# One product per unit of the narrow feed-forward parts issued in two column pieces

## The chip, the cores and the metric

The kernel runs on one core of one Trainium2 chip. The metric is the device time of one execution in microseconds (us).

## What is computed

Two transformer-like blocks run one after the other on one sequence of 256 tokens with 1024 channels. The first has four layers, each with a mixer (retention, convolution, dilated attention, retention) and a gated feed-forward part; the second has two layers over 272 tokens (16 tokens are put ahead), each with a mixer and a wider feed-forward part. The change is in the feed-forward parts of the first block, four times this:

```python
DEPTH = 4
FFN_HIDDEN = -(-8 * D_MODEL // (3 * 256)) * 256          # 2816

def _swiglu(h, w_in, w_out):
    a = h @ w_in
    return (jax.nn.silu(a[..., :FFN_HIDDEN]) * a[..., FFN_HIDDEN:]) @ w_out

def first_block(x, ...):
    for i in range(DEPTH):
        hn = _rmsnorm(x, norm_w[i, 0])
        ...
        x = x + _rmsnorm(m, norm_w[i, 1])
        f = _swiglu(_rmsnorm(x, norm_w[i, 2]), ffn_w_in[i], ffn_w_out[i])
        x = x + _rmsnorm(f, norm_w[i, 3])
    return x
```

## The kernel before, in words

Activations lie with channels on the 128 partitions and tokens (256, or 272 in the second block) along the columns. Every dense matrix is a `Phase`: it is cut into units, and a unit is `tiles` weight tiles of 128x128 that are multiplied into one output of 128 channels. For each layer of the first block there are two feed-forward phases, whose names begin with `ffn`: `ffn_in` with 44 units of 8 tiles (gate and value rows in pairs), and `ffn_out` with 16 units of 11 tiles, two units per output. The second block's feed-forward phases are called `mlp_in` and `mlp_out`; they stream 272 columns and are not touched.

SyncE (SP) loads one unit's weights at a time into a ring of raw slots. ScalarE (line 1313) rounds four tiles at a time to `weights_hi` (type fp32r), VectorE (line 2155) puts the remainder into `weights_lo`, and adds to the semaphore `split_ready`. The activations are split likewise into a high and a low part. TensorE then makes each dense product out of three fp32r products, in `product`: hi by hi (line 526), weight hi by activation lo (line 527), and weight lo by activation hi (line 528), all accumulated in the same PSUM bank. The stationary operand is the 128x128 weight tile, the moving one the activations of all 256 tokens.

`multiply` runs one unit: for each tile k it calls `product`, waits on `split_ready` at every fourth tile, and tells the splitting engines through `sub_multiplied` when four tiles are done. In `ffn_in` the first four units go through `first_units`, tile by tile as the normalised activations arrive, which calls `product` by itself; the other 40 units go through `multiply`, four of them in `turn(1, False)` and 36 in a hardware loop of nine rounds with four units each. `ffn_out` goes through `dense` in four rounds of four units. The order on each engine is that of the code; semaphores alone tie the engines together.

Other products in the kernel (attention scores, norm sums, transposes) have F32 operands, not fp32r. The filler `keep_busy` (line 520) and line 578 are such.

Of the kernel before, what the change touches and what calls it, by code (L numbers as in the profile page):

```python
# [44 lines left out]
SLOTS = 4  # L45
SUB = 4
SUBS = 4
SLOT_TILES = 11


# [151 lines left out]
def build(nc, dram, out, const_at):  # L202
# [3 lines left out]
    with ExitStack() as ctx:  # L206
        def sb(name, shape):
            return ctx.enter_context(nc.sbuf_tensor(name, shape, F32))

        def sbr(name, shape):  # L210
            return ctx.enter_context(nc.sbuf_tensor(name, shape, F32R))
# [4 lines left out]

        raw = [sb(f"weights{s}", [P, SLOT_TILES, P]) for s in range(SLOTS)]
        w_hi = [sbr(f"weights_hi{s}", [P, SUB, P]) for s in range(SUBS)]
        w_lo = [sbr(f"weights_lo{s}", [P, SUB, P]) for s in range(SUBS)]
        h = sb("h", [P, DC, S2])  # L220
# [293 lines left out]
        def _(pe):  # L514
# [4 lines left out]
                for _ in range(n):  # L519
                    nc.tensor.matmul(PS[:, bank, 0:S1], mean, rope_cos[:, 0:S1], start=True, stop=True)  # L520

            def product(acc, hi, lo, src, first, last):


                src_hi, src_lo = src
                nc.tensor.matmul(acc, hi, src_hi, start=first, stop=False)  # L526
                nc.tensor.matmul(acc, hi, src_lo, start=False, stop=False)  # L527
                return nc.tensor.matmul(acc, lo, src_hi, start=False, stop=last)  # L528

            def multiply(phase, i, u, acc, src, ready=None):  # L530


                for k in range(phase.tiles):
                    kk = (u % phase.upo) * phase.tiles + k
                    sub = u * phase.sps + k // SUB
                    if k % SUB == 0:
                        pe.wait_ge(split_ready, i * (phase.body * phase.sps) + (phase.sub0 + sub + 1))
                    if ready:
                        pe.wait_ge(*ready(kk))
                    last = product(acc, w_hi[sub % phase.subs][:, k % SUB, :], w_lo[sub % phase.subs][:, k % SUB, :], src(kk),  # L540
                                   kk == 0, kk == phase.upo * phase.tiles - 1)
                    if k % SUB == SUB - 1 or k == phase.tiles - 1:
                        last.then_inc(sub_multiplied, 1)

            def dense(phase, src, n, free, first_free, ready, begin=0):


                body = phase.body
                banks = SLOTS if phase.upo == 1 else 2
                with pe.Fori(begin, phase.units // body) as i:  # L550
                    for u in range(body):
                        o = u // phase.upo
                        if phase.pairs:
                            if u % 2 == 0:
                                pe.wait_ge(free, i * (body // 2) + (first_free + u // 2))
                        elif u % phase.upo == 0:
                            pe.wait_ge(free, i * (body // phase.upo) + (first_free + o))
                        multiply(phase, i, u, PS[:, o % banks, 0:n], src, ready if u < phase.upo else None)

            def last_outputs(phase, src, n):  # L560

                for u in range(phase.body):
                    multiply(phase, 1, u, PS[:, 4 + u, 0:n], src)
# [27 lines left out]
            def first_units(phase, src, ready, acc=lambda u: PS[:, 4 + u, 0:S1]):  # L591

                for c in range(DC):
                    pe.wait_ge(split_ready, phase.sub0 + c + 1)
                    pe.wait_ge(*ready(c))
                    for u in range(4):
                        last = product(acc(u), w_hi[c % phase.subs][:, u, :], w_lo[c % phase.subs][:, u, :], src(c),
                                       c == 0, c == DC - 1)
                    last.then_inc(sub_multiplied, 1)
# [12 lines left out]
            def ret_queries(phase, layer, src, ready):  # L612
                first_units(phase, src, ready)
                pe.wait_ge(out_evacuated, FREE_BANKS + phase.out0)
                multiply(phase, 1, 0, PS[:, 0, 0:S1], src)
                if layer == 0:
                    pe.wait_ge(consts_loaded, 16)
                input_mean(2 * layer)
                multiply(phase, 1, 1, PS[:, 1, 0:S1], src)
                multiply(phase, 1, 2, PS[:, 2, 0:S1], src)  # L620
                pe.wait_ge(rstd_ready, 4 * layer + 1)
                multiply(phase, 1, 3, PS[:, 3, 0:S1], src)
                pe.wait_ge(out_evacuated, evacuated(phase, 4))
                turn_row(2 * layer, 4)
                dense_outputs(phase, src, S1, None, 2)
# [29 lines left out]
            def retention(j, layer):  # L655
# [27 lines left out]
                def part_output(sub, o, quarter):  # L683

                    pe.wait_ge(split_ready, phase.sub0 + sub + 1)
                    for k in range(SUB):
                        pe.wait_ge(R["split"], ret_split(j, SUB * quarter + k))
                        last = product(PS[:, 4 + o, 0:S1], w_hi[sub % phase.subs][:, k, :], w_lo[sub % phase.subs][:, k, :],
                                       (ret_hi[SUB * quarter + k], ret_lo[SUB * quarter + k]),
                                       quarter == k == 0, quarter == SUB - 1 and k == SUB - 1)  # L690
                    last.then_inc(sub_multiplied, 1)
# [541 lines left out]
            def normed(number, n):  # L1233

                return (lambda k: (xn_hi[n][:, k, :], xn_lo[n][:, k, :])), (lambda k: (x_split, DC * number + k + 1))

            def hidden(hi, lo, name):
                return (lambda k: (hi[:, k, :], lo[:, k, :])), (lambda k: (part_lo, hidden0[name] + k + 1))

            for layer in range(DEPTH):  # L1240
# [6 lines left out]
                src, ready = normed(2 * layer, S1)  # L1247
# [20 lines left out]
                src, ready = normed(2 * layer + 1, S1)  # L1268
                gated_pairs(ph[f"ffn_in{layer}"], layer, src, ready)
                src, ready = hidden(hid_hi, hid_lo, f"ffn_in{layer}")  # L1270
# [3 lines left out]
            for layer in range(2):  # L1274
                src, ready = normed(2 * DEPTH + 2 * layer, S2)
# [8 lines left out]
                src, ready = normed(2 * DEPTH + 2 * layer + 1, S2)  # L1284
                dense_outputs(ph[f"mlp_in{layer}"], src, S2, ready)
                post_sum(17 + 2 * layer, S2)
                src, ready = hidden(mlp_hi, mlp_lo, f"mlp_in{layer}")
# [2205 lines left out]
```

## Time and profile before

| | |
|---|---|
| median of 2 runs | 2409.32 us (2403.69 to 2414.94) |
| the profiled execution's own time | 2417.55 us |
| its span, first to last instruction | 2415.8 us |
| mean granted TensorE clock | 0.999 |
| TensorE matmul busy | 2375.3 us, 98% of the span |
| TensorE weight load busy | 2279.6 us, 94% |
| VectorE, ScalarE busy | 1705.2 us, 1359.8 us |

Two rows of TensorE are shown: PE is the streaming of the moving operand, PEld the load of the stationary one, which can run beside the streaming of the instruction before. The duration of one PE record reaches past the start of the next, because matmuls are pipelined; what an instruction costs in a stream is the distance between two starts (called the pitch below), not its duration.

### The profile page before, as it was taken

The numbers are of one execution on the slowest core, as the hardware profiler recorded it, in microseconds if no ns is written. First come the engines' busy times: TensorE is split into PE (matmuls) and PEld (weight loads), VectorE is DVE, ScalarE is ACT, GpSimd is POOL, SyncE is SP. The second block draws the span as 40 slices with busy tenths as digits, with TensorE's granted clock in tenths as the row PEclk, the third lists the DMA queues.
The fourth block names the chain that finished last, engine by engine and source line by source line (L and its number), as shares of the span: only waits on it lengthen the run. The fifth ranks groups of instructions, "written<-read, shape, count | busy, mean of one in ns | idle before, by whom it ended". The sixth has DMA issues, their size and how long they took to land.

```text
span 2415.8 us, 55632 instructions
## 1 busy us (share of the span) xinstructions
PE 2375.3 (98%) x20004; PEld 2279.6 (94%) x20004; DVE 1705.2 (71%) x3359; ACT 1359.8 (56%) x2806; POOL 3.4 (0%) x9
## 2 busy tenths in 40 slices
PE   8999999999999999999999999999999999999998
PEld 8899999889999999999998999999899999999998
DVE  7666767877658778776576667657576776677864
ACT  5555555465556555565555565557755444566544
POOL 0000000000000000000000000000000000000000
PEclk9999999999999999999999999999999999999999
DMA  7635664335654444455655446645444555434564
GB/s 238 175 122 163 193 201 155 107 106 178 196 166 141 132 144 138 139 160 187 203 157 174 139 148 190 204 163 160 133 139 131 171 178 180 132 111 141 175 179 134
DMA packets 103400, 385.75 MB, mean 160 GB/s; under 512 B 11344, under 2 KB 13520, under 8 KB 103024
## 3 DMA queue, kind: packets, MB, share of 16 engines
q1 hardware_dynamic: 102784, 381.78, 51.1%
q0 software_dynamic: 496, 2.38, 0.3%
q8 instruction: 73, 1.20, 0.2%
q14 instruction: 47, 0.39, 0.0%
HBM read 383.07 MB, written 1.05 MB: 159 GB/s over the span
## 4 chain that ended last, share of the span: by engine, by line
PE 90%; DVE 6%; ACT 2%; issue 1%; DMA 0%; DVEq 0%; ACTq 0%; SPq 0%
PE acc L526 26%; PE acc L527 25%; PE acc L528 25%; DVE weights_lo L2155 2%; PE acc L732 1%; PE acc L734 1%; PE acc L733 1%; ACT weights_hi L1313 1%; PE acc L754 1%; PE acc L821 1%; DVE h L2304 1%; DVE y L2293 1%; DVE xn_parts L2300 1%; PE acc L844 1%; PE acc L866 1%
## 5 line engine op out<-in xcount | busy, mean ns | idle before, releaser
L2155 DVE TENSOR_TENSOR weights_lo<-weights,weights_hi 128x512 fp32r<-128x512 f32 (+1 forms) x1392 | 907.2, 682 | 405.8 <-ACT weights_hi L1313 400.6
L526 PE MATMUL acc<-xn_parts,weights_hi 128*128 128x256 f32 (+1 forms) x3456 | 986.2, 285 | 15.1 <-DVE xn_parts L2300 6.9
L527 PE MATMUL acc<-xn_parts,weights_hi 128*128 128x256 f32 (+1 forms) x3456 | 971.8, 281 | 0.0
L528 PE MATMUL acc<-xn_parts,weights_lo 128*128 128x256 f32 (+1 forms) x3456 | 971.6, 281 | 0.0
L1313 ACT ACTIVATE weights_hi<-weights 128x512 fp32r<-128x512 f32 (+1 forms) x1392 | 815.7, 620 | 259.3 <-PE acc L528 229.7
L526 PEld LDWEIGHTS acc<-xn_parts,weights_hi 128*128 128x128 f32 x3456 | 653.2, 189 | 32.0 <-issue 22.7
L528 PEld LDWEIGHTS acc<-xn_parts,weights_lo 128*128 128x128 f32 x3456 | 651.5, 189 | 0.0
L527 PEld LDWEIGHTS acc<-xn_parts,weights_hi 128*128 128x128 f32 x3456 | 650.4, 188 | 0.9
L526 PE MATMUL acc<-arena_r,weights_hi 128*128 128x256 f32 (+1 forms) x1792 | 510.0, 285 | 3.6 <-DVE arena_r L2796 1.2
L528 PE MATMUL acc<-arena_r,weights_lo 128*128 128x256 f32 (+1 forms) x1792 | 506.3, 283 | 0.0
L527 PE MATMUL acc<-arena_r,weights_hi 128*128 128x256 f32 (+1 forms) x1792 | 506.2, 282 | 0.0
L526 PEld LDWEIGHTS acc<-arena_r,weights_hi 128*128 128x128 f32 x1792 | 338.2, 189 | 6.7 <-issue 3.3
L527 PEld LDWEIGHTS acc<-arena_r,weights_hi 128*128 128x128 f32 x1792 | 337.9, 189 | 0.3
L528 PEld LDWEIGHTS acc<-arena_r,weights_lo 128*128 128x128 f32 x1792 | 337.6, 188 | 0.0
L1574 ACT ACTIVATE y<-y 128x256 f32<-128x256 f32 x88 | 35.9, 416 | 158.6 <-DVE y L2469 158.6
L2469 DVE TENSOR_TENSOR y<-acc,rstd 128x256 f32<-128x256 f32 x88 | 36.6, 423 | 73.5 <-PE acc L528 73.5
L1952 ACT ACTIVATE silu<-acc 128x272 f32<-128x272 f32 x64 | 25.5, 398 | 96.0 <-PE acc L528 95.9
L526 PE MATMUL acc<-xn_parts,arena_r 128*128 128x256 f32 (+1 forms) x256 | 74.1, 290 | 0.5 <-DVE xn_parts L2300 0.4
L528 PE MATMUL acc<-xn_parts,arena_r 128*128 128x256 f32 (+1 forms) x256 | 71.7, 280 | 0.0
L527 PE MATMUL acc<-xn_parts,arena_r 128*128 128x256 f32 (+1 forms) x256 | 71.7, 280 | 0.0
L2271 DVE TENSOR_TENSOR sum_of_squares<-sum_of_squares,sq 128x256 f32<-128x256 f32 (+1 forms) x79 | 33.9, 429 | 49.0 <-ACT sq L1399 33.9
L1755 ACT ACTIVATE arena<-acc 128x256 f32<-128x256 f32 x63 | 23.5, 374 | 62.4 <-PE acc L528 62.4
(325 smaller groups left out, 2324.3 us busy)
## 6 DMA issues: line engine op xcount, KB each, us to landing
weights<-in_ffn_in SPq DMA_DIRECT2D x176, 512.0 KB, 3.8
weights<-in_ffn_out SPq DMA_DIRECT2D x64, 704.0 KB, 4.1
weights<-in_att_in SPq DMA_DIRECT2D x72, 512.0 KB, 3.5
weights<-in_mlp_in SPq DMA_DIRECT2D x64, 512.0 KB, 3.5
weights<-in_mlp_out SPq DMA_DIRECT2D x64, 512.0 KB, 3.5
weights<-in_ret_qk SPq DMA_DIRECT2D x32, 512.0 KB, 3.9
weights<-in_ret_v SPq DMA_DIRECT2D x32, 512.0 KB, 3.7
weights<-in_ret_g SPq DMA_DIRECT2D x32, 512.0 KB, 3.5
```

Of the source, the lines that this page charges most:

```text
L526: nc.tensor.matmul(acc, hi, src_hi, start=first, stop=False)
L527: nc.tensor.matmul(acc, hi, src_lo, start=False, stop=False)
L528: return nc.tensor.matmul(acc, lo, src_hi, start=False, stop=last)
L732: nc.tensor.matmul(acc, x_hi[:, tokens], whi, start=(k == 0), stop=False)
L733: nc.tensor.matmul(acc, x_hi[:, tokens], wlo, start=False, stop=False)
L734: last = nc.tensor.matmul(acc, x_lo[:, tokens], whi, start=False, stop=(k == DC - 1))
L1313: nc.scalar.activation(w_hi[sub % phase.subs][:, 0:n, :], raw[slot][:, j * SUB:j * SUB + n, :], ACT.Copy)\
L1574: nc.scalar.activation(ffn_gate[:, slot, :], ffn_gate[:, slot, :], ACT.Silu).then_inc(gate_ready, 1)
L1952: nc.scalar.activation(silu[:, u % 2, :], PS[:, u % SLOTS, 0:S2], ACT.Relu).then_inc(out_evacuated, 1)
L2155: nc.vector.tensor_tensor(w_lo[sub % phase.subs][:, 0:n, :], raw[slot][:, j * SUB:j * SUB + n, :], w_hi[sub % phase.subs][:, 0:n, :].bitca ...
L2271: nc.vector.tensor_tensor(ssum[:, 0:n], ssum[:, 0:n], sq[:, o, 0:n], ALU.add).then_inc(y_added, 1)
L2469: nc.vector.tensor_tensor(ffn_gate[:, slot, :], acc, rstd[:, 0:S1], ALU.mult).then_inc(gate_scaled, 1)
```

## The change

`product` gets an argument `cut`. Where it is not zero, the middle product (weight hi by activation lo) is issued as two instructions with the same weight tile: one for the columns up to `cut`, one for the rest. `multiply` passes it for tile k = 2 of each unit of a phase whose name begins with `ffn`: 240 for the first unit of a round (240+16 columns), 128 for the second (128+128), 192 for the third (192+64), 252 for the fourth (252+4). The columns that are multiplied stay the same in number and content.

```diff
+CUTS = (240, 128, 192, 252)
...
-            def product(acc, hi, lo, src, first, last):
+            def product(acc, hi, lo, src, first, last, cut=0):
 
 
                 src_hi, src_lo = src
                 nc.tensor.matmul(acc, hi, src_hi, start=first, stop=False)
-                nc.tensor.matmul(acc, hi, src_lo, start=False, stop=False)
+                if cut:
+                    nc.tensor.matmul(acc[:, 0:cut], hi, src_lo[:, 0:cut], start=False, stop=False)
+                    nc.tensor.matmul(acc[:, cut:], hi, src_lo[:, cut:], start=False, stop=False)
+                else:
+                    nc.tensor.matmul(acc, hi, src_lo, start=False, stop=False)
                 return nc.tensor.matmul(acc, lo, src_hi, start=False, stop=last)
...
                     last = product(acc, w_hi[sub % phase.subs][:, k % SUB, :], w_lo[sub % phase.subs][:, k % SUB, :], src(kk),
-                                   kk == 0, kk == phase.upo * phase.tiles - 1)
+                                   kk == 0, kk == phase.upo * phase.tiles - 1,
+                                   CUTS[u] if k == 2 and phase.name.startswith("ffn") else 0)
```

TensorE in `ffn_in0`, the first unit after the tile-by-tile start, tiles 1 to 3 of its first four tiles, before (`xn_parts` are the split activations, `weights_hi0` and `weights_lo0` the first buffer of split weights):

```order
L526 MATMUL acc<-xn_parts,weights_hi0 128x256
L527 MATMUL acc<-xn_parts,weights_hi0 128x256
L528 MATMUL acc<-xn_parts,weights_lo0 128x256
L526 MATMUL acc<-xn_parts,weights_hi0 128x256
L527 MATMUL acc<-xn_parts,weights_hi0 128x256
L528 MATMUL acc<-xn_parts,weights_lo0 128x256
L526 MATMUL acc<-xn_parts,weights_hi0 128x256
L527 MATMUL acc<-xn_parts,weights_hi0 128x256
L528 MATMUL acc<-xn_parts,weights_lo0 128x256
```

The same place after the change:

```order
L527 MATMUL acc<-xn_parts,weights_hi0 128x256
L532 MATMUL acc<-xn_parts,weights_hi0 128x256
L533 MATMUL acc<-xn_parts,weights_lo0 128x256
L527 MATMUL acc<-xn_parts,weights_hi0 128x256
L529 MATMUL acc<-xn_parts,weights_hi0 128x240
L530 MATMUL acc<-xn_parts,weights_hi0 128x16
L533 MATMUL acc<-xn_parts,weights_lo0 128x256
L527 MATMUL acc<-xn_parts,weights_hi0 128x256
L532 MATMUL acc<-xn_parts,weights_hi0 128x256
L533 MATMUL acc<-xn_parts,weights_lo0 128x256
```

The middle product of tile 2 stands there as two rows of 240 and 16 columns; its neighbours are as before (lines 526, 527 and 528 are now 527, 532 and 533).

TensorE in `ffn_out0`, the fourth unit of the round, tiles 1 to 3, before (`arena_r_50` holds the split hidden activations):

```order
L528 MATMUL acc<-arena_r_50,weights_lo1 128x256
L526 MATMUL acc<-arena_r_50,weights_hi1 128x256
L527 MATMUL acc<-arena_r_50,weights_hi1 128x256
L528 MATMUL acc<-arena_r_50,weights_lo1 128x256
L526 MATMUL acc<-arena_r_50,weights_hi1 128x256
L527 MATMUL acc<-arena_r_50,weights_hi1 128x256
L528 MATMUL acc<-arena_r_50,weights_lo1 128x256
L537 REGISTER_ALU
```

The same place after the change:

```order
L532 MATMUL acc<-arena_r_50,weights_hi1 128x256
L533 MATMUL acc<-arena_r_50,weights_lo1 128x256
L527 MATMUL acc<-arena_r_50,weights_hi1 128x256
L529 MATMUL acc<-arena_r_50,weights_hi1 128x252
L530 MATMUL acc<-arena_r_50,weights_hi1 128x4
L533 MATMUL acc<-arena_r_50,weights_lo1 128x256
L527 MATMUL acc<-arena_r_50,weights_hi1 128x256
L532 MATMUL acc<-arena_r_50,weights_hi1 128x256
L533 MATMUL acc<-arena_r_50,weights_lo1 128x256
```

Here the pieces have 252 and 4 columns. In the whole program TensorE has 7345 rows written in place of 7297, 48 more: eight places in each of four `ffn_in` phases and four in each of four `ffn_out` phases. The other engines' instructions are unchanged.

## Rows read from the trace of the kernel before

**Rows 1.** Page of the profile: span, busy time, and the chain by engine and line.

```profile
span 2415.8 us, 55632 instructions
...
PE 2375.3 (98%) x20004; PEld 2279.6 (94%) x20004; DVE 1705.2 (71%) x3359; ACT 1359.8 (56%) x2806; POOL 3.4 (0%) x9
...
PE 90%; DVE 6%; ACT 2%; issue 1%; DMA 0%; DVEq 0%; ACTq 0%; SPq 0%
PE acc L526 26%; PE acc L527 25%; PE acc L528 25%; DVE weights_lo L2155 2%; PE acc L732 1%; PE acc L734 1%; PE acc L733 1%; ACT weights_hi L1313 1%; PE acc L754 1%; PE acc L821 1%; DVE h L2304 1%; DVE y L2293 1%; DVE xn_parts L2300 1%; PE acc L844 1%; PE acc L866 1%
...
```

**Rows 2.** Page, costliest groups: the three products, loads included, and both weight splits.

```profile
...
L2155 DVE TENSOR_TENSOR weights_lo<-weights,weights_hi 128x512 fp32r<-128x512 f32 (+1 forms) x1392 | 907.2, 682 | 405.8 <-ACT weights_hi L1313 400.6
L526 PE MATMUL acc<-xn_parts,weights_hi 128*128 128x256 f32 (+1 forms) x3456 | 986.2, 285 | 15.1 <-DVE xn_parts L2300 6.9
L527 PE MATMUL acc<-xn_parts,weights_hi 128*128 128x256 f32 (+1 forms) x3456 | 971.8, 281 | 0.0
...
L1313 ACT ACTIVATE weights_hi<-weights 128x512 fp32r<-128x512 f32 (+1 forms) x1392 | 815.7, 620 | 259.3 <-PE acc L528 229.7
...
L527 PEld LDWEIGHTS acc<-xn_parts,weights_hi 128*128 128x128 f32 x3456 | 650.4, 188 | 0.9
...
```

**Rows 3.** Windows: inside ffn_in0, ffn_out0, ffn_in1, ffn_out1 (us, busy and instruction counts).

```profile
core 0: us, PE busy (x) PEld busy (x) DVE busy (x) ACT busy (x) POOL busy (x), PEclk, DMA share, GB/s
238.50:344.50 106.00, 106.00 (x936) 106.00 (x937) 74.53 (x144) 61.48 (x124) 0.00 (x0) 1.00 0.66 197
344.80:406.80 62.00, 61.72 (x525) 61.52 (x524) 39.88 (x64) 33.74 (x64) 0.00 (x0) 1.00 0.55 179
551.50:661.50 110.00, 110.00 (x936) 110.00 (x935) 74.48 (x144) 61.27 (x123) 0.00 (x0) 1.00 0.62 193
661.80:723.80 62.00, 61.97 (x526) 61.77 (x526) 34.30 (x57) 33.94 (x64) 0.00 (x0) 1.00 0.52 166
```

**Rows 4.** Waits in 222 to 344 us, norm and ffn_in0 (us, times, longest).

```profile
...
ACT weights_hi L1313 <- PE acc L528: 8.0, 22, 0.8
PEld acc L526 <- issue: 2.7, 4, 1.7
...
PE acc L526 <- DVE xn_parts L2300: 1.6, 2, 1.4
PEld acc L526 <- DVE weights_lo L2155: 0.3, 1, 0.3
...
```

**Rows 5.** Waits in 344.7 to 407 us, ffn_out0.

```profile
...
ACT weights_hi L1313 <- PE acc L528: 22.7, 34, 1.0
...
PEld acc L526 <- DVE weights_lo L2155: 0.5, 1, 0.5
PE acc L526 <- DVE weights_lo L2155: 0.3, 1, 0.3
```

**Rows 6.** Timeline at 310 us, ffn_in0: start us, us, engine, instruction.

```profile
...
309.90 0.28 PE L526 MATMUL acc<-xn_parts,weights_hi 128*128 128x256 f32 x1
309.91 0.19 PEld L527 LDWEIGHTS acc<-xn_parts,weights_hi 128*128 128x128 f32 x1
310.02 0.28 PE L527 MATMUL acc<-xn_parts,weights_hi 128*128 128x256 f32 x1
310.02 0.19 PEld L528 LDWEIGHTS acc<-xn_parts,weights_lo 128*128 128x128 f32 x1
310.13 0.28 PE L528 MATMUL acc<-xn_parts,weights_lo 128*128 128x256 f32 x1
310.13 0.19 PEld L526 LDWEIGHTS acc<-xn_parts,weights_hi 128*128 128x128 f32 x1
...
310.24 0.28 PE L526 MATMUL acc<-xn_parts,weights_hi 128*128 128x256 f32 x1
...
```

**Rows 7.** Timeline of weight loads at 2101.54 us, in windows ending 2101.60, 2101.70, 2101.82.

```profile
2101.54 0.19 PEld L1115 LDWEIGHTS acc<-small,arena 80*128 80x128 f32 x1 [0.33 <-issue]
...
2101.54 0.30 PEld L1115 LDWEIGHTS acc<-small,arena 80*128 80x128 f32 x2 [0.33 <-issue]
...
2101.54 0.41 PEld L1115 LDWEIGHTS acc<-small,arena 80*128 80x128 f32 x3 [0.33 <-issue]
```

**Rows 8.** Line 1115, F32, 16 columns streamed: ns min/median/max, forms.

```profile
...
L1115 PEld LDWEIGHTS acc<-small,arena x48: 92/189/192, 2101.5 to 2191.8; 80*128 80x128 f32 x32, 80*16 80x16 f32 x16
L1115 PE MATMUL acc<-small,arena x48: 176/262/283, 2101.5 to 2191.8; 80*128 80x16 f32 x32, 80*16 80x16 f32 x16
...
```

**Rows 9.** Timeline: F32 products of 256 columns (line 650) and 128 columns (line 578).

```profile
101.37 1.89 PE L650 MATMUL acc<-arena 128*128 128x256 f32 x8
...
1628.55 0.38 PE L578 MATMUL acc<-const_a 128*128 128x128 f32 x2
```

**Rows 10.** Groups by form: F32 of 128 columns, and fp32r of 512 columns.

```profile
...
L732 PE MATMUL acc<-weights_hi,xn_parts 128*128 128x512 f32 x128 | 50.5, 394 | 0.0
...
L578 PE MATMUL acc<-const_a 128*128 128x128 f32 x14 | 2.7, 274 | 0.0
...
```


## The prediction

> **What bounds the kernel now.** I read the page first. TensorE streams during 98% of the span, its weight loads cover 94%, and it holds 90% of the chain that ended last; the three lines of `product` alone hold 76% [rows 1]. The reader should see that nothing else comes near: VectorE is at 71% and ScalarE at 56%. The groups say why they idle: the split on VectorE waits for the one on ScalarE, and that waits for TensorE (229.7 us of 259.3), since the buffers come free only when TensorE has used them [rows 2].
>
> Then the stages that the change touches. Inside `ffn_in0` TensorE started 936 matmuls in 106.0 us and was never idle, inside `ffn_in1` 936 in 110.0 us; `ffn_out0` and `ffn_out1` show 525 and 526 records in 62.0 us [rows 3]. So the pitch is 113.2 ns in `ffn_in0`, 117.5 in `ffn_in1`, 118.0 in `ffn_out`. VectorE is busy 74.5 us of the 106.0 and ScalarE 61.5; the DMA engines are at 0.66. In the waits, TensorE lost 0.3 us to weights in `ffn_out0` and none in the whole of `ffn_in0`; its loads waited 0.3 and 0.5 us [rows 4, 5]. It is ScalarE that waits for TensorE there, 8.0 and 22.7 us. Whatever lengthens TensorE's stream in these phases lengthens the program by as much, and whatever makes the others faster gives nothing.
>
> Last, how one product follows another [rows 6]. The load of L527's weights starts with the streaming of L526, the streaming of L527 starts 0.11 us after that, and with it the next load. Each load can thus run beside one streaming only, the one just ahead of it. L526 and L527 use the same tile of `weights_hi`, and it is loaded for both: PE and PEld have the same count, 20004 [rows 1], and the group of L527 has 3456 loads to 3456 matmuls [rows 2].
>
> **The change, part by part.**
>
> *How many.* Per layer `ffn_in` cuts 40 units (44 less the 4 of `first_units`, which passes no cut), `ffn_out` cuts 16. Four layers make 4 x 56 = 224 cut products, 56 of each kind. There are 224 more matmuls and, if the rule of the rows holds, 224 more weight loads. Columns streamed, PSUM banks, semaphore waits and signals stay the same; no DMA, no split and no evacuation is added or moved. The list of instructions shows one row turned into two and nothing else. All of this other work costs nothing.
>
> *What a piece costs.* No fp32r product of fewer than 256 columns is in the trace, so the price comes from neighbours. Line 1115 has products that load 128 weight columns and stream only 16. Its first loads show in windows that end later and later: one load ends at 0.19 us, two at 0.30, three at 0.41 [rows 7]. So they follow each other every 0.11 us, though only 16 columns are streamed with each. The load's duration is the same as that of our products, 189 ns against 188 [rows 8, 2]. I read it so: a 128-column load needs some 0.11 us however little is streamed beside it, and at 256 columns stream and load are nearly equally long. A piece of 240, 192, 128, 64, 16 or 4 columns then costs one load, 0.110 to 0.113 us; I take 112 ns.
>
> *The sum.* A cut product costs 2 x 112 = 224 ns in place of one pitch.
> - `ffn_in`, two layers like `ffn_in0` (80 products; which two hardly matters): 80 x (224 - 113.2) = 8.9 us.
> - `ffn_in`, two layers like `ffn_in1`: 80 x (224 - 117.5) = 8.5 us.
> - `ffn_out`: 64 x (224 - 118.0) = 6.8 us.
>
> Together 24.2 us. With 110 ns a piece it is 23.3 us, with 113.2 it is 24.7, and if the 256-column pitch of 118 held for each piece too it would be 224 x 0.118 = 26.4. All of it is on the path, by the waits above. What may come back is what TensorE waited for weights in these phases: under 0.5 us each, so under 4 us for all eight by the two shown; I give nothing back.
>
> Against the profiled execution's own 2417.55 us this is 2441.8. That execution lies 0.3% above the median of the runs, 2409.32, and above both of them, so I put the sum on the median: 2409.3 + 24.2 = 2433.5 us, +1.0%.
>
> *A rule against this.* By [rows 7] a product that streams 16 columns costs as much as a load of 128. The Trainium skill (TensorE: Matmul & The Clock Gate, "LDWEIGHTS (loading the stationary operand)") says that a load takes as many cycles of 1.2 GHz as it has weight columns, which is 107 ns for 128: the rows agree. The same page, "Back-to-back issue gap", gives a gap by streamed columns alone, N/2.4 + 2.5 ns and never under about 25 ns; by that 128+128 costs 2 ns more than 256 and 252+4 some 24 ns more, about 12 ns on average, and the change 3 us. It also states a sustained 81 ns for 128 columns with loads between, which would make two pieces 162 ns and the change about 10 us. Rows 7 speak against both for this kernel's loads.
>
> **Rivals.**
>
> *The narrow pieces fall to the rate of F32: slower by over 2%.* Every product in the trace with fewer than 256 columns has F32 operands; every fp32r one has 256, 272 or 512 [rows 2, 10]. So it is open whether an fp32r product keeps its one pass when it is narrow. An F32 product costs much more: line 578 is written 7 times in the run and has 14 records, two each [rows 10], and a record of 256 columns has a pitch of (1.89 - 0.38)/7 = 0.216 us (line 650), one of 128 columns 0.38 - 0.27 = 0.11 us [rows 9, 10]. That is 0.84 ns a column in each of two records, with a floor of one load. Priced so, 240+16 costs 2 x 203 + 2 x 112 = 629 ns, 128+128 costs 448, 192+64 548 and 252+4 650: 569 on average in place of 117, 224 x 0.452 = 101.2 us, 2511 us. If it is one record at four times the column time (1.69 ns a column, floor 112), the four cost 518, 432, 436 and 538, 481 on average, and 224 x 0.364 = 81.5 us, 2491 us. It decides above 2% as soon as a cut product costs 48.2/224 = 0.215 us more than before, that is over 0.33 us. Half the rate (0.84 ns a column in one record) would be 315, 224, 274 and 325 ns, mean 285, and +38 us, 2447. For it: the missing narrow fp32r rows. Against it: an fp32r record in the trace looks like any other, one load and one stream, and I see nothing in it that would depend on the count of columns.
>
> *The second piece finds its weights loaded: no change.* If the load of a tile that is already there were left out, the pieces would cost their columns and a few ns: +1 to +3 us, 2410 to 2412. Against it stands that L527 loads the very tile of L526 before it [rows 2, 6]. If the load is made but half of it is hidden behind the two streamings, the change costs half the sum, +12 us, 2421; [rows 7] show no such hiding.
>
> *The cover.* If TensorE waited for weights in these units, the extra time would be hidden. The waits in [rows 4, 5] exclude more than 4 us, so this only shaves the forecast to about 2430.
>
> *Faster* has no mechanism: columns and waits are the same, loads only come on top. Only drift between runs could show it.
>
> **How the numbers follow.** The load-bound piece (with or without the small cover) gets 0.75, 2428 to 2440 with the spread of the medians. The F32 rate gets 0.15 (2491 to 2511), half rate 0.02 (2447). The free second piece gets 0.04, the half-hidden load 0.03, drift to the faster side 0.01. The likeliest is 2433.5. For 8 in 10 the range takes in the load bound, the half rate, and the cheap cases: 2411 to 2449. A measurement of this kernel can tell about 2% from no change, which is 48 us. Slower by over 2% holds the F32 rate alone, 0.15; faster by over 2% the drift, 0.01; within 2% are all the others, 0.84.
>
> **What would show it.** In the profile after, PE and PEld counts both rise by about 224. In `ffn_in` the two records of a cut product start some 0.11 us apart, whichever of the four cuts it is, 4 columns like 240, and a load stands between them. `ffn_in` becomes longer by 40 x 0.11 = 4.3 to 4.4 us, `ffn_out` by 1.7 us, and all other phases stay. The pitch of uncut products, the clock and the waits for weights stay too, while ScalarE's wait for TensorE grows a little. If the F32 rate holds, the 128+128 pair is the cheapest and 252+4 the dearest, pitches of 0.2 us or more show behind the wide pieces, and perhaps two records each. If the load is spared, the 4-column piece has a pitch of a few tens of ns. The prediction is wrong if a narrow fp32r product is not bound by its load, or if it costs the products around it something too.

## The result and the profile after

The changed kernel takes 2430.72 us (median of 2 runs, 2430.01 to 2431.43) against 2409.32 before: ratio 1.0077, 95% interval 1.0052 to 1.0101. In a second group of runs it was 2429.90 us (2429.71 to 2431.10) against 2404.76 (21 runs, 2402.70 to 2407.15): ratio 1.0107, interval 1.0091 to 1.0122. The change makes the kernel slower by about 1%. One execution of the kernel before, among the 12 of a later control, took 6021.68 us for a reason that the record doesn't show; no ratio counts it.

The page of the changed kernel, its span, busy times, chain and two of the costliest groups:

```profile
span 2428.2 us, 56080 instructions
...
PE 2387.8 (98%) x20228; PEld 2291.9 (94%) x20228; DVE 1704.9 (70%) x3359; ACT 1360.1 (56%) x2806; POOL 3.4 (0%) x9
...
PE 89%; DVE 7%; ACT 3%; issue 1%; DMA 0%; DVEq 0%; ACTq 0%; SPq 0%
...
L1319 ACT ACTIVATE weights_hi<-weights 128x512 fp32r<-128x512 f32 (+1 forms) x1392 | 815.7, 619 | 266.7 <-PE acc L533 238.8
L532 PE MATMUL acc<-xn_parts,weights_hi 128*128 128x256 f32 (+1 forms) x3296 | 924.7, 281 | 0.0
...
```

Beside [rows 1, 2]: both counts of TensorE rise by 224, from 20004 to 20228, so each piece is one matmul record with one load of its own. The span rises by only 12.4 us, and the busy time of PE by 12.5, where 224 loads of 0.112 us would be 25. ScalarE waits 9.1 us longer for TensorE's last product (229.7 to 238.8); nobody else's work changes.

The groups by form (shape, count, then busy us and mean ns) show the pieces of `ffn_in`:

```profile
...
L530 PE MATMUL acc<-xn_parts,weights_hi 128*128 128x128 f32 x40 | 11.0, 276 | 0.0
L529 PE MATMUL acc<-xn_parts,weights_hi 128*128 128x252 f32 x40 | 11.0, 274 | 0.0
L529 PE MATMUL acc<-xn_parts,weights_hi 128*128 128x240 f32 x40 | 10.8, 269 | 0.0
...
L529 PE MATMUL acc<-xn_parts,weights_hi 128*128 128x192 f32 x40 | 9.9, 248 | 0.0
...
L529 PE MATMUL acc<-xn_parts,weights_hi 128*128 128x128 f32 x40 | 8.8, 220 | 0.0
L530 PE MATMUL acc<-xn_parts,weights_hi 128*128 128x64 f32 x40 | 8.7, 218 | 0.0
...
L530 PE MATMUL acc<-xn_parts,weights_hi 128*128 128x16 f32 x40 | 7.1, 177 | 0.0
L530 PE MATMUL acc<-xn_parts,weights_hi 128*128 128x4 f32 x40 | 6.7, 167 | 0.0
...
```

The durations rise with the columns: as the first piece (L529) 220, 248, 269 and 274 ns for 128, 192, 240 and 252 columns, as the second (L530) 167, 177, 218 and 276 ns for 4, 16, 64 and 128. The first pieces give (274 - 220)/124 = 0.44 ns a column, half of the 0.84 that the prediction read for one record of F32, so a narrow fp32r product is neither split in two records nor slower by the column. With 128 columns the second piece takes 276 ns where the first takes 220: more than the columns is in a duration, and it is no price. The timeline around a 252+4 cut in `ffn_in0` (start, duration in us) gives that:

```profile
...
279.14 0.28 PE L527 MATMUL acc<-xn_parts,weights_hi 128*128 128x256 f32 x1
279.15 0.19 PEld L529 LDWEIGHTS acc<-xn_parts,weights_hi 128*128 128x128 f32 x1
279.26 0.27 PE L529 MATMUL acc<-xn_parts,weights_hi 128*128 128x252 f32 x1
279.26 0.19 PEld L530 LDWEIGHTS acc<-xn_parts,weights_hi 128*128 128x128 f32 x1
279.37 0.17 PE L530 MATMUL acc<-xn_parts,weights_hi 128*128 128x4 f32 x1
279.37 0.19 PEld L533 LDWEIGHTS acc<-xn_parts,weights_lo 128*128 128x128 f32 x1
279.39 0.36 PE L533 MATMUL acc<-xn_parts,weights_lo 128*128 128x256 f32 x1
...
279.48 0.19 PEld L527 LDWEIGHTS acc<-xn_parts,weights_hi 128*128 128x128 f32 x1
279.60 0.28 PE L527 MATMUL acc<-xn_parts,weights_hi 128*128 128x256 f32 x1
...
```

The reader should follow the PEld rows alone: loads start at 279.15, 279.26, 279.37, 279.48, that is every 0.11 us, with the cut or without. The 4-column piece and the product behind it (L533) have recorded starts only 0.02 us apart, but L533's load began at 279.37 and the next one began 0.11 us later, as behind all others, and L533's record is 0.36 long in place of 0.28. I read it so: the record begins before its weights are there. L527 then starts 0.20 us after L533 (200 ns in the unrounded starts). A 128+128 cut looks different and comes to the same up to this point:

```profile
...
273.56 0.22 PE L529 MATMUL acc<-xn_parts,weights_hi 128*128 128x128 f32 x1
273.57 0.19 PEld L530 LDWEIGHTS acc<-xn_parts,weights_hi 128*128 128x128 f32 x1
273.62 0.28 PE L530 MATMUL acc<-xn_parts,weights_hi 128*128 128x128 f32 x1
273.67 0.19 PEld L533 LDWEIGHTS acc<-xn_parts,weights_lo 128*128 128x128 f32 x1
273.73 0.33 PE L533 MATMUL acc<-xn_parts,weights_lo 128*128 128x256 f32 x1
...
273.79 0.19 PEld L527 LDWEIGHTS acc<-xn_parts,weights_hi 128*128 128x128 f32 x1
273.90 0.28 PE L527 MATMUL acc<-xn_parts,weights_hi 128*128 128x256 f32 x1
...
```

Here the second piece starts 0.05 to 0.06 us after the first, L533 0.11 later, and L527 0.17 later; from the first piece to L527 it is 0.34 us for three instructions, as above. The unrounded starts show a difference behind that. After a 252+4 or 240+16 cut the next products follow at 113 to 114 ns, after 128+128 or 192+64 the next three at about 117, 119 and 116 ns and the rest at 113 to 114. Summed up to the next cut, the first two kinds cost 113 ns a cut over the pitch, the last two 126.

The stages, in windows that answer to [rows 3] (inside `ffn_in0`, `ffn_out0`, `ffn_in1`, `ffn_out1`; a window also counts the two or three matmuls that are in progress where it begins):

```profile
core 0: us, PE busy (x), PEclk, DMA share, GB/s
238.50:349.00 110.50, 110.50 (x972) 1.00 0.62 190
350.00:411.00 61.00, 60.95 (x536) 1.00 0.53 177
557.00:667.00 110.00, 110.00 (x971) 1.00 0.62 191
668.00:729.00 61.00, 60.94 (x537) 1.00 0.51 168
```

`ffn_in0` has 972 in 110.5 us, 113.7 ns each, near its 113.2 of before. But `ffn_in1` has 971 in 110.0 us, and had 936 in 110.0 [rows 3]: its pitch fell from 117.5 to about 113.3 ns. In the same way 536 fit in 61.0 us of `ffn_out0`, where 525 took 62.0. The waits in `ffn_in0` answer to [rows 4] and are the same but for ScalarE's:

```profile
...
ACT weights_hi L1319 <- PE acc L533: 10.4, 24, 0.9
...
PE acc L527 <- DVE xn_parts L2306: 1.6, 2, 1.4
PEld acc L527 <- DVE weights_lo L2161: 0.3, 1, 0.3
...
```

So the profile holds two things: 224 bare loads, about +25 us, and a shorter pitch in five of the eight feed-forward phases, about -15 us; the remaining 1.5 us lie in other phases. Which of them is the change's own had to be found out. By the two spans alone, 12.4 us apart, the prediction's rival of a half-hidden load (+12 us) would fit as well.

### The profile page after: what moved, and what is told of

Same layout as the page of the kernel before. It is cut to its first block, busy times and chain, and to the rows that moved or that the text cites. A ratio compares the mean times of both kernels' runs of the same rounds, so it can differ in the third digit from the quotient of the medians.

```text
span 2428.2 us, 56080 instructions
## 1 busy us (share of the span) xinstructions
PE 2387.8 (98%) x20228; PEld 2291.9 (94%) x20228; DVE 1704.9 (70%) x3359; ACT 1360.1 (56%) x2806; POOL 3.4 (0%) x9
## 4 chain that ended last, share of the span: by engine, by line
PE 89%; DVE 7%; ACT 3%; issue 1%; DMA 0%; DVEq 0%; ACTq 0%; SPq 0%
PE acc L527 25%; PE acc L533 25%; PE acc L532 24%; DVE weights_lo L2161 2%; PE acc L738 1%; PE acc L740 1%; PE acc L739 1%; ACT weights_hi L1319 1%; PE acc L760 1%; PE acc L827 1%; PE acc L529 1%; DVE h L2310 1%; DVE y L2299 1%; PE acc L850 1%; PE acc L872 1%
## 5 line engine op out<-in xcount | busy, mean ns | idle before, releaser
L527 PE MATMUL acc<-xn_parts,weights_hi 128*128 128x256 f32 (+1 forms) x3456 | 983.4, 285 | 15.0 <-DVE xn_parts L2306 7.0
L533 PE MATMUL acc<-xn_parts,weights_lo 128*128 128x256 f32 (+1 forms) x3456 | 981.3, 284 | 0.0
L1319 ACT ACTIVATE weights_hi<-weights 128x512 fp32r<-128x512 f32 (+1 forms) x1392 | 815.7, 619 | 266.7 <-PE acc L533 238.8
L532 PE MATMUL acc<-xn_parts,weights_hi 128*128 128x256 f32 (+1 forms) x3296 | 924.7, 281 | 0.0
L527 PEld LDWEIGHTS acc<-xn_parts,weights_hi 128*128 128x128 f32 x3456 | 652.1, 189 | 31.9 <-issue 22.6
L533 PEld LDWEIGHTS acc<-xn_parts,weights_lo 128*128 128x128 f32 x3456 | 650.4, 188 | 0.0
L532 PEld LDWEIGHTS acc<-xn_parts,weights_hi 128*128 128x128 f32 x3296 | 620.3, 188 | 0.9
L527 PE MATMUL acc<-arena_r,weights_hi 128*128 128x256 f32 (+1 forms) x1792 | 507.9, 283 | 3.3 <-DVE arena_r L2802 1.2
L533 PE MATMUL acc<-arena_r,weights_lo 128*128 128x256 f32 (+1 forms) x1792 | 509.3, 284 | 0.0
L532 PE MATMUL acc<-arena_r,weights_hi 128*128 128x256 f32 (+1 forms) x1728 | 486.4, 281 | 0.0
L527 PEld LDWEIGHTS acc<-arena_r,weights_hi 128*128 128x128 f32 x1792 | 337.1, 188 | 6.4 <-issue 3.3
L533 PEld LDWEIGHTS acc<-arena_r,weights_lo 128*128 128x128 f32 x1792 | 337.7, 188 | 0.0
L532 PEld LDWEIGHTS acc<-arena_r,weights_hi 128*128 128x128 f32 x1728 | 325.4, 188 | 0.3
L527 PE MATMUL acc<-xn_parts,arena_r 128*128 128x256 f32 (+1 forms) x256 | 74.0, 289 | 0.5 <-DVE xn_parts L2306 0.4
L533 PE MATMUL acc<-xn_parts,arena_r 128*128 128x256 f32 (+1 forms) x256 | 71.7, 280 | 0.0
L1761 ACT ACTIVATE arena<-acc 128x256 f32<-128x256 f32 x63 | 23.5, 374 | 62.5 <-PE acc L533 62.5
```

Source lines behind the costliest of these rows:

```text
L1319: nc.scalar.activation(w_hi[sub % phase.subs][:, 0:n, :], raw[slot][:, j * SUB:j * SUB + n, :], ACT.Copy)\
```

## The experiments

All times are medians of device time; the kernel before, run beside each group, is named with it. The runs came in three groups (the first four, the next four, the last three), each on another chip. "Phase length" is the time from the first to the last start of `product`'s matmuls in a phase of the profiled execution. For `ffn_in` it is taken over the unbroken row of units at its end, 936 products without cuts: the tile-by-tile start and one unit more stand before it, and with that unit one of the 40 cuts, so 39 lie inside. All 16 cuts of an `ffn_out` lie inside.

**Twice the cuts.** Tile 6 of each unit is cut too.

```diff
-                                   CUTS[u] if k == 2 and phase.name.startswith("ffn") else 0)
+                                   CUTS[u] if k in (2, 6) and phase.name.startswith("ffn") else 0)
```

> Cuts tile 6 of each unit too: 448 cut products in place of 224. Theory A (a cut costs one more weight load, 113 ns; and after a cut TensorE goes from its 118 ns pitch to its 113.4 ns pitch, which the changed kernel has gained in its feed-forward phases already): 25.4 us longer than the changed kernel's profile, a span of 2453 us, all feed-forward phases at about 113.7 ns per record. Theory B (no pitch is regained, a cut costs 21.4/224 = 96 ns or less): 12 to 21 us longer, span 2441 to 2450.

Measured 2457.78 us, against 2405.68 for the kernel before (ratio 1.021, 1.0197 to 1.0223), 27 us over the changed kernel. Span 2456.0. `ffn_in` phases take 115.5 us, `ffn_out` 63.7, all eight alike. Against phases that had the short pitch without any cut (106.1 and 60.3 us, next run) that is 9.4/78 = 120 ns and 3.4/32 = 106 ns a cut: a fixed price of about one load for each. In `ffn_out` the cuts also shorten a wait: early in the phase, where TensorE waits for split weights, two starts lie 0.56 us apart in the run without cuts and 0.21 here; with these 0.35 us it is 117 ns a cut. The span lies at the side of theory A, 3 us above it, and 6 us beyond the upper end of B's.

**The kernel before again**, no edit.

> The kernel before again, for a second profile. Theory A: a phase's pitch is one of two values, 113.4 or 118 ns, and holds to the end of the phase; if it hangs on how the phase begins, the same phases can have the other one in this execution, and the span differs from 2415.8 by multiples of about 4 us (ffn_in) and 2 us (ffn_out). Rival: the same phases have the same pitch, and the span is 2415.8 within 1 us.

Measured 2405.66 us (12 executions, that of 6021.68 among them; kernel before 2405.68, ratio 0.9998, 0.9987 to 1.0008), span 2403.4 in the profile, 12.4 us less than in the profile from which I predicted. The windows inside `ffn_in0`, `ffn_out0`, `ffn_in1`, `ffn_out1` of this execution:

```profile
238.00:343.50 105.50, 105.50 (x934) 1.00 0.65 198
344.50:404.00 59.50, 59.22 (x522) 1.00 0.56 183
551.00:656.50 105.50, 105.50 (x934) 1.00 0.66 198
658.00:717.00 59.00, 58.71 (x518) 1.00 0.53 175
```

All eight feed-forward phases have the short pitch: 106.1 us for each `ffn_in` and 60.3 for each `ffn_out`. In the first profile it was 106.1, 110.2, 110.2, 106.1 and 62.5, 62.4, 60.2, 62.5. The pitch of a phase can thus differ from one execution to the next of the same program, and the rival (same phases, same pitch) fell.

**One cut per phase or round**, 20 in all.

```diff
-                                   CUTS[u] if k == 2 and phase.name.startswith("ffn") else 0)
+                                   252 if (phase.name.startswith("ffn_in") and isinstance(i, int) and u == 3 and k == 6)
+                                   or (phase.name.startswith("ffn_out") and u == 2 and k == 2) else 0)
```

> 20 cuts of 252+4 in place of 224: one per ffn_in phase behind its start, one per round in ffn_out. Theory A: ffn_in1 and ffn_in2 go from 110.2 to about 106.5 us, each ffn_out from 62.4 to about 60.9, while ffn_in0 and ffn_in3 stay at 106.1 plus 0.1: span 2415.8 - 7.5 - 5 = about 2403 us, ratio 0.994 to 0.998. Rival (which phase has which pitch is chance of a run and not set by a cut): the phases keep their pitches or change without order, span 2415.8 + 2.3 = 2418, ratio 1.000 to 1.002.

Measured 2407.40 us against 2405.68 (ratio 1.0001, 0.9989 to 1.0013), span 2406.8. All four `ffn_in` took 106.2 us and all `ffn_out` 60.7, as theory A said. The ratio did not come down and lies in the rival's range, since the kernel before mostly had the short pitch by itself in that group of runs. In this profile all 20 cuts came upon products that had the short pitch already, so the run is no test of A.

**A short load for the narrow piece.** All cuts 252+4; 32 of 128 weight columns for the 4-column piece.

```diff
-                    nc.tensor.matmul(acc[:, cut:], hi, src_lo[:, cut:], start=False, stop=False)
+                    nc.tensor.matmul(acc[0:32, cut:], hi[:, 0:32], src_lo[:, cut:], start=False, stop=False)
```

> All 224 cuts are 252+4, and the 4-column piece is multiplied with 32 of the 128 weight columns only, so its load is a quarter as long; the contribution of the other 96 output channels for these 4 columns is left out. Theory A (the load is the price): a cut costs some 28 ns above the 113.4 ns pitch, 6 us in all, and since the pitch of 118 is given up after a cut, the span comes out below that of the kernel before, 2403 to 2411 us. Rival (the price is a fixed cost of one more matmul instruction or of the turn to other columns): a cut costs 113 ns as in the changed kernel, span about 2428.

Measured 2429.42 us against 2405.68 (ratio 1.0095, 1.0082 to 1.0108). The time fell on the rival's side: the short load gave nothing. The timeline shows why my expectation was badly formed:

```profile
...
244.49 0.27 PE L529 MATMUL acc<-xn_parts,weights_hi 128*128 128x252 f32 x1
244.49 0.11 PEld L530 LDWEIGHTS acc<-xn_parts,weights_hi 128*32 128x32 f32 x1
...
244.60 0.17 PE L530 MATMUL acc<-xn_parts,weights_hi 128*32 128x4 f32 x1
244.60 0.19 PEld L533 LDWEIGHTS acc<-xn_parts,weights_lo 128*128 128x128 f32 x1
244.63 0.36 PE L533 MATMUL acc<-xn_parts,weights_lo 128*128 128x256 f32 x1
244.71 0.19 PEld L527 LDWEIGHTS acc<-xn_parts,weights_hi 128*128 128x128 f32 x1
244.83 0.28 PE L527 MATMUL acc<-xn_parts,weights_hi 128*128 128x256 f32 x1
...
```

The short load (0.11 long in place of 0.19) stands beside the 252-column stream, where even a full one is hidden. The load that stands beside the 4-column stream is the one of L533, still 128 columns: L533's load starts at 244.60 and the next load 0.11 later. That gave theory C: a step costs the longer of one instruction's stream and the next one's load. The next three runs set it against the rival that a matmul has a fixed price.

**The narrow piece first, 4+252.** `CUTS = (4, 4, 4, 4)`.

> All 224 cuts are 4+252: the narrow piece comes first. Theory C (formed on the run before this one: each step costs the longer of the stream of one instruction and the load of the next, and a load of 128 columns takes 108 to 113 ns): the load of the 252-column piece stands beside 4 columns of streaming and is bare, so a cut costs 108 to 113 ns as at 252+4, 2430 us against 2405.7. Rival (the fixed price lies in what follows a narrow last piece, since the product behind it starts 200 ns before its successor): a cut becomes cheaper, below 60 ns, under 2419 us.

Measured 2429.58 us, phase lengths 110.5 and 61.9: (110.5 - 106.1)/39 = 113 ns a cut. The run before this one, with 252+4, has the same two lengths. In `ffn_out` it is 1.6/16 = 99 ns, and 113 with the 0.23 us that the wait for weights became shorter (0.56 to 0.33).

**4+252 with a short load for the second piece.** The edits of the two runs above together.

> As 4+252, but the 252-column piece is multiplied with 32 of the 128 weight columns, so that its own load, the one that stands beside 4 columns of streaming, is a quarter as long; what the other 96 output channels would get from it is left out. Theory C: a cut costs 27 to 40 ns, 6 to 9 us in all, 2412 to 2415 us. Rival (a fixed cost of one more matmul, whatever its load): 113 ns a cut, 2430 us.

Measured 2419.34 us. Each `ffn_in` takes 107.4 us: (107.4 - 106.1)/39 = 33 ns a cut, in theory C's range and a third of the rival's 113. The time lies 4 us above the range, and the phases say where that comes from: `ffn_out0` took 60.8 us, the other three 62.9. Those three took the pitch of 118 ns at the wait for weights behind their first unit, and none of the 15 cuts behind it ended it. With a short load a cut of this kind doesn't bring the short pitch.

**252+4 with a short load for the product behind it.**

```diff
+                if cut:
+                    return nc.tensor.matmul(acc[0:32, :], lo[:, 0:32], src_hi, start=False, stop=last)
                 return nc.tensor.matmul(acc, lo, src_hi, start=False, stop=last)
```

> Cuts 252+4, and the product behind the cut (weight lo by activation hi) is multiplied with 32 of its 128 weight columns, so that the load beside the 4-column stream is short; its other 96 output channels are left out. Theory C: 27 to 40 ns a cut, 2412 to 2415 us, and the load of the 4-column piece itself stays 128 columns long. Rival (fixed cost per matmul): 2430 us.

Measured 2412.10 us, phase lengths 107.4 and 60.8, that is 33 and 31 ns a cut. The timeline of one:

```profile
...
320.65 0.27 PE L529 MATMUL acc<-xn_parts,weights_hi 128*128 128x252 f32 x1
320.65 0.19 PEld L530 LDWEIGHTS acc<-xn_parts,weights_hi 128*128 128x128 f32 x1
...
320.76 0.17 PE L530 MATMUL acc<-xn_parts,weights_hi 128*128 128x4 f32 x1
320.77 0.11 PEld L534 LDWEIGHTS acc<-xn_parts,weights_lo 128*32 128x32 f32 x1
320.79 0.28 PE L534 MATMUL acc<-xn_parts,weights_lo 128*32 128x256 f32 x1
320.80 0.19 PEld L527 LDWEIGHTS acc<-xn_parts,weights_hi 128*128 128x128 f32 x1
320.91 0.28 PE L527 MATMUL acc<-xn_parts,weights_hi 128*128 128x256 f32 x1
...
```

The 4-column stream (L530, with its full load at 320.65) now has the short load of L534 beside it, and the next load starts 0.03 us later, not 0.11. L527 starts 0.26 us after the wide piece, where it was 0.34. The count of matmuls is the same as in the changed kernel; 80 of the 113 ns went with 96 weight columns. The short load of the first run of this kind stood beside the wide stream and gave nothing, here it stands beside the narrow one and gives 80 ns: the fixed price fell, the bare load stands.

In this group (these three runs and the next) the kernel before ran at 2415.91 us (29 runs, 2407.84 to 2424.53), 10 us above the other groups, while the 4+252 kernel with a cut in every unit stayed within 2428.74 to 2430.35. The times of the three are therefore read against each other and by their phases, not by their ratios (1.0049, 1.0014 and 0.9977 in the order shown; the last kernel leaves out part of the products, its cuts cost 7 us in all, and its feed-forward phases had the short pitch, which the kernel before, to go by its time, mostly had not).

**Cuts where the long pitch is steady.** No cut in `ffn`; one per round in the third unit of `ret_g`, `ret_out` (252+4) and of the `mlp` phases (256+16).

```diff
-                                   CUTS[u] if k == 2 and phase.name.startswith("ffn") else 0)
+                                   (252 if phase.name.startswith(("ret_g", "ret_out")) else 256) if u == 2 and k == 2
+                                   and phase.name.startswith(("ret_g", "ret_out", "mlp")) else 0)
```

> No cut in the ffn phases; one cut per round, in its third unit, in ret_g and ret_out (252+4) and in the mlp phases of the second block (256+16). Theory A (after a cut TensorE keeps the 113.4 ns pitch until something halts it): ret_g goes from 45.3 to about 43.8 us and ret_out's 360 products from 42.5 to about 41.3, twice each; for the mlp phases, whose pitch of 124 ns has no second value in any trace so far, either 120 ns, 3 us less per phase, or as before plus 0.9 us per phase: span 2398 at best, 2402 without the gain in mlp. Rival (the pitch of 118 ns in ret_g and ret_out comes from what the other engines do or where the operands lie): these phases stay at 118 ns and each cut costs 0.11 us, span 2403 to 2410.

Measured 2416.12 us against 2415.91 (ratio 0.9992, 0.9980 to 1.0005). In `ret_out0`, where every other profile with no cut there has 118.3 ns throughout, the first cut comes at 188.7 us. One window ahead of it and two behind:

```profile
core 0: us, PE busy (x), PEclk, DMA share, GB/s
174.00:187.00 13.00, 13.00 (x113) 1.00 0.50 140
190.00:199.00 9.00, 9.00 (x82) 1.00 0.55 167
200.00:209.00 9.00, 9.00 (x82) 1.00 0.60 183
```

Less the two or three matmuls in progress at each window's start, that is 13.0/110.6 = 118 ns ahead and 9.0/79.6 = 113 ns behind, and it lasts to the end of the phase. The phase took 41.8 us in place of 42.5. In `ret_out3` the first cut changed nothing and the second did, 42.2 us. The last run below has these cuts too, on another chip, and shows the same: 41.8 and 42.2 us, short from the first and from the second cut on. In the 11 profiles without cuts there all 22 of these phases took 42.47 us. Here the change of pitch is the cut's own work. In `ret_g` little was won (45.1 and 44.7 against 45.2 and 45.0), since the long pitch can come back at a wait before the next cut; the 43.8 expected did not come. The `mlp` phases got 0.9 us longer with 8 cuts and 0.5 with 4, 110 to 115 ns a cut, at the same 124 ns pitch: with 272 columns no second pitch showed. The untouched `ffn` phases had the long pitch in six of eight here, with no cut to end it; that is why the profile's span, 2418.9, lies outside both ranges of the expectation.

**The changed kernel, the 20 cuts, and the 20 with those of the retention phases**, beside each other.

> The changed kernel again, in rounds beside the kernel before. Theory A: its feed-forward phases hold the 113.4 ns pitch in every execution, so it lies at 2429 to 2432 us whatever the chip, with a spread of 3 us or less, while the kernel before lies between 2402 and 2424 by the pitches it happens to have; the ratio is 1.010 where the latter has the short pitch, down to 1.005 where not. Rival (the ratio is a property of the kernels alone): 1.0077 as first measured, and equal spreads.

> The 20 cuts of the run e3_once again. Theory A: as there, the eight feed-forward phases at 106.2 and 60.7 us in the profile, and 2405 to 2410 us on any chip; against a kernel before that is at 2416 on its chip this is 0.996, against one at 2405.7 it is 1.000. Rival (a cut in one place of a phase does not hold): spread and median as those of the kernel before, plus 2 us.

> The 20 cuts of e3_once and one per round in ret_g and ret_out. Theory A: ret_g 45.0 and ret_out 42.0 us, together 1.5 us less than without; 2403 to 2409 us, that is 0.994 to 1.000 of the kernel before by what pitches that one has. Rival: cuts in the retention phases cost 0.11 us each and give nothing, 2 us longer than f2_once.

Measured against 2404.76 us: the changed kernel 2429.90 (1.0107, 1.0091 to 1.0122), the 20 cuts 2407.55 (1.0011, 1.0002 to 1.0020), those and the retention's 2406.84 (1.0009, 1.0000 to 1.0018). The changed kernel's lengths were again 110.8 and 62.0 in all phases, its spread was 1.4 us, and the 1.0077 of the rival lies outside the interval. In both others every `ffn_in` took 106.2 to 106.5 us and every `ffn_out` 60.8. No version beats the kernel before where that has the short pitch anyway; the cuts then cost their own 2 us. What the 20 cuts do on the chip where the long pitch was common was not run. In the run with them alone all 20 again met the short pitch, and its time and spread (5.5 us, the kernel before 4.5) suit its rival as well. With the retention's cuts the last `ffn_in` came to its one cut with the long pitch and left it with the short one. The third expectation's 1.5 us less than without is 0.7, inside the spread; its `ret_out` phases came down as expected, its `ret_g` phases, at 45.6 and 44.8, by nothing that can be told from the spread of the runs without cuts there (44.9 to 45.4).

## Why the prediction was right

**What bounds the kernel** held: 224 loads more on TensorE and little wait given back, 0.23 us in each `ffn_out`, 0.9 in all, where I had allowed up to 4 and put it at nothing; the other engines' busy times are the same within 0.4 us.

**The price of a piece and the sum** held: a piece was to cost 112 ns, so that a cut adds 111 to a product of 113.4. The `ffn_in` phases give 113 for the cuts 252+4, 240+16 and 4+252, and 120 for the mixture of four. Summed over the phases against those of the control: 4 x 4.7 + 4 x 1.7 = 25.6 us. The forecast was +24.2; the medians give +25.0 and +25.1 against a kernel before at 2405.7 and 2404.8 (the first of the two from another group of runs), and +21.4 against the two runs first shown. The predicted 2433.5 us is 3 us high, because it was put on a median that holds executions with the long pitch. That it comes so near is in part luck: the two runs of the kernel before lay at 2403.69 and 2414.94, and the base could have been anywhere between. The phase lengths carry the price, not this agreement.

**The reason for the price** was shown and not only argued: a load beside 4 columns of stream is bare, and with a quarter of its columns the cut costs 33 ns. What it doesn't explain are the 13 ns more of 128+128 and 192+64, which lie on the products behind the cut. The prediction named a cost to the products around as a sign that it is wrong; for half of the cuts there is one, a ninth of their price, and its cause stays open. One sentence of the reason was right in [rows 6] and forgotten in the run with the short load: the load beside a narrow stream is that of the instruction behind.

**The sign of it in the timeline** was half wrong. I expected the records of a cut 0.11 us apart for all cuts. The loads are; the matmul records are 0.03 to 0.11 apart, by the columns, and the delay shows one product later, which is followed only 0.17 to 0.20 us after its start.

**The pitch stays** was wrong. I took 113.2 ns in `ffn_in0` and 117.5 and 118.0 elsewhere for properties of the phases (and 118.0 for every `ffn_out` by the two that I had looked at; `ffn_out2` had the short one, 60.2 us). They are two values that one phase can have in different executions, and with a cut in every unit and full loads all phases had the short one. With the short pitch in all, the sum would have been 224 x 224 ns less 224 x 113.4, 24.8 us. The error is small in the sum and large in the picture: comparing the two profiles alone, 12.4 us, would have given half the price.

**The rivals.** The F32 rate fell at once: one record each, 0.44 ns a column, and 128+128 is not the cheapest of the four but 13 ns dearer than 252+4. The loaded tile that is not loaded again fell by the counts. The half-hidden load (+12 us) would have been confirmed by the two first profiles alone, and fell by the control's phases (+25.6) and by twice the cuts (27 us more). The Trainium skill (TensorE: Matmul & The Clock Gate, "Back-to-back issue gap") gives a product of N columns N/2.4 + 2.5 ns by its columns alone, 56 ns for 128, and states 81 ns for 128 columns in a stream with loads. In the 128+128 cut two such products and the one behind them took 340 ns, 113 each, so neither figure describes these pieces. By the recorded starts alone 252+4 would seem to follow the column rule, with 0.11 and 0.02 us; the product behind pays for it.

## What to carry to other kernels

With 128x128 fp32r weights a product of 256 columns just covered the next load here, at 113.4 ns; each of the cuts measured left one full load more uncovered, 0.11 us, wherever the cut lay and whatever the duration of its records said. Cost a split by the loads that stand beside its streams, and read it from the PEld starts, never from the distance of two matmul records. Before two profiles are subtracted, compare the pitch in phases that the change leaves alone or that repeat: here an accident of the first profile was over half as large as the effect.

## What the runs showed of the hardware that was not expected

The same stream of fp32r products of 256 columns ran at 113.4 or at about 118 ns per product, at a granted clock of 0.999 to 1.0 in every profile. The pitch changed only where the stream was broken, by a wait or by a cut: of over 2000 unbroken stretches of 13 products or more in the 13 profiles none holds both behind its first few products, and the longest have over 900. At waits it changed both ways, in over half of some 450 cases. So a whole `ffn_in` has the pitch that it takes at the one break at its start. Of the 24 `ffn` phases in the three profiles without cuts there (the kernel before, its control, the run with cuts elsewhere) 13 had the short pitch by their length. Of the 72 in the nine profiles with cuts there, the one with 4+252 and a short load left out, all 72 had it by their length, though 23 of the 24 with one cut per phase or round met their first cut with it already. Counted over the ten profiles with cuts (again without 4+252 and a short load), 43 cuts came upon the long pitch, and 27 of them were followed by the short one. Some 1600 came upon the short one, and none of them was followed by the long one. That is how a phase with a cut in every unit comes to the short pitch and stays there. With 4+252 and a short load 1 of 48 did it. Why a cut works in one direction only, and what gives a stretch the long pitch in the first place, was not found and stays open. Neither did it pay: one cut costs what some 25 products win by it.

The spread of the times fits this. With a cut in every unit the changed kernel stayed within 1.4 us in each group; the kernel before ranged over 17 us in two groups and 4.5 us in the third. Its median differs too, 2415.9 in the group of the second chip and 2405.7 and 2404.8 in the others; whether that is the chip's doing or the hour's was not tried.
